# The S5 products of a hybrid decoder layer: from the accumulators to two spare banks, as one block behind each dense tile

## The chip, the cores and the metric

The kernel runs on one core of one Trainium2 chip. Its time is the device time of one execution in microseconds. Before the change the median of three runs is 2421.3 us (2419.39 to 2423.79). The engines are TensorE (PE), VectorE (DVE), ScalarE (ACT), GpSimd (POOL) and SyncE (SP, which here only issues DMAs). Each works off its own queue in order, and they meet by semaphores.

## The reference

One inference step of a two-layer decoder trunk over 1024 prompt rows and 8 x 4 sample rows, 1056 columns in all (T), model width 1024. Layer 0 is the even one, which the change concerns:

```python
p = rmsnorm(x, g_norm) @ w_in                      # q, k, v, g, a_lr, u
log_a = log_sigmoid(a_lr @ w_a2 + b_a2) / 16
o, s_gla = gla_chunked(q, k, v, log_a, s_gla)      # 4 heads
o = rmsnorm(o, g_head) * silu(g)
# S5: 32 groups of 16 channels, 64 complex states each
bu = einsum('bsgc,gpc->bsgp', u, bb)               # complex
h  = scan(h[t] = ab * h[t-1] + bu[t])              # complex, along the sequence
y  = Re(einsum(h, c)) + d_skip * u
z = gelu(y); z = z * sigmoid(z @ w_glu + b_glu)
x = x + concat([o, z]) @ w_out
x = x + square(relu(rmsnorm(x, g_mlp) @ w_up)) @ w_down
```

Layer 1 has a gated RG-LRU in the mixer's place, and the same MLP.

## The kernel before, in words

Everything lies with channels on the 128 partitions and the 1056 columns along the free axis. A dense product is done in three passes on two rounded halves of each operand (XH, XL for the activations, WH, WL for a weight tile of 128 x 1024): `product` runs 8 k steps x 3 column chunks of 352 x 3 passes, 72 matmuls, into one of two accumulators of three banks each (`acc[:, t % 2]`). Names are numbered in the table ACC; tile t may start when t - 2 has been read (`claim`). The weight tiles come in the order of the table STREAM; for each, ScalarE copies the raw tile to WH (`hi(n)`) and VectorE subtracts to get WL (`lo_w(n)`), which TensorE awaits. Two further banks, `ms`, are spare.

The even layer projects u0 to u3, q0, q1, g0 to g3, k0, k1, alr and the three tiles v0 to v2 (these with 512 columns; k runs over four weight tiles, n = 13 to 16). The S5 part works on four groups q = 0 to 3 of eight channel groups each, between the dense tiles. For each group: `build_xa` on VectorE, `step_ab` on TensorE (8 transposes and 12 products of 32 columns) which ScalarE reads to WIN and T7 (`read_ab`); `load_m`, eight small DMAs that spread T7 to M; `step_cd` (16 half-array products of 136 columns), read by `read_cd`; `core` on VectorE, the scan itself, with the angle tables built by `build_angles` and turned to sine and cosine by `turn_table`; `build_wo`; `step_ef` (24 products of 136 columns), read by `read_ef` to G. Then y goes out to DRAM (`store_y`), comes back turned (`turn_y`, eight DMAs), ScalarE does the GELU into TT[:, 2] and SP stores z (`z_out`). Both `decay` steps, which make the GLA decays out of the logits lg0 and lg1, wait on VectorE for `z_out` of all four groups and on ScalarE for the g stores. After them VectorE runs a long series of steps up to `pair_carried(0)`, then the weight tiles 17 and 18 and the low halves of z, which the first GLU tile on TensorE waits for. ScalarE's queue is written out by hand, as are VectorE's and TensorE's; their order sets what waits for what.

## Time and profile before

| | |
|---|---|
| median of 3 runs | 2421.3 us (2419.39 to 2423.79) |
| profiled execution | 2420.45 us, span 2418.6 us |
| mean granted TensorE clock | 0.956 of full |
| TensorE busy | 2337.1 us, 97% of the span |
| VectorE busy | 1188.8 us, 49% |
| ScalarE busy | 648.9 us, 27% |

The profile is of one execution, times counted from its first instruction. PE is TensorE's matmul row; a line such as L488 is that of a helper that many steps share, so steps are told apart by the tiles that they write and read (acc<-U,WIN is cd, ms or acc<-U,M opens ef, cst,XA is ab's transposes). The clock is given as a share: 1.00 is 2.4 GHz and 0.50 is 1.2 GHz. A number in brackets at a row's end is the idle time of the engine ahead of it, with what ended it. Some matmul records are missing from the trace.

### The profile page before, as it was taken

How to read it: one execution, taken by the hardware profiler on the slowest of the kernel's cores; microseconds unless marked ns; L12 is line 12 of the kernel's file. 1: busy time of each engine (PE TensorE's matmuls, PEld its weight loads, DVE VectorE, ACT ScalarE, POOL GpSimd, SP SyncE). 2: the span in 40 equal slices, each digit the busy share in tenths (PEclk: the TensorE clock that was granted, in tenths of full speed). 3: DMA queues.
4: the chain of work that ended last, by engine and by line, in shares of the span. 5: the costliest groups of instructions: out<-in, count | busy, mean ns of one | idle time of the engine just before them, and what ended most of it. 6: DMA issues, size and time to landing. Idle time of an engine off the chain costs nothing.

```text
span 2418.6 us, 32428 instructions
## 1 busy us (share of the span) xinstructions
PE 2337.1 (97%) x14010; PEld 2263.1 (94%) x14010; DVE 1188.8 (49%) x1324; ACT 648.9 (27%) x708; POOL 21.0 (1%) x35
## 2 busy tenths in 40 slices
PE   7999979989999999999999999999999999999997
PEld 6988768789999999999999888899999999999996
DVE  7874545234434434444446866624444444344344
ACT  5232432133211111112113544614211111111113
POOL 0000000000000000000000000000000000000001
PEclk9988985599999999999999999999999999999999
DMA  4343110131111111111111111111111111111112
GB/s 158 99 111 104 71 44 19 35 118 44 48 49 46 39 52 43 43 52 43 43 52 36 49 40 48 33 52 44 44 43 52 43 43 52 44 43 37 51 34 72
DMA packets 66087, 131.62 MB, mean 54 GB/s; under 512 B 24400, under 2 KB 37344, under 8 KB 66016
## 3 DMA queue, kind: packets, MB, share of 16 engines
q1 hardware_dynamic: 60256, 114.88, 14.7%
q0 software_dynamic: 3312, 12.06, 1.5%
q10 hardware_dynamic: 2448, 3.64, 0.5%
q8 instruction: 56, 0.92, 0.2%
q14 instruction: 15, 0.12, 0.0%
HBM read 114.66 MB, written 14.71 MB: 53 GB/s over the span
## 4 chain that ended last, share of the span: by engine, by line
PE 90%; DVE 5%; ACT 2%; issue 1%; DMA 1%; SPq 0%; DVEq 0%; ACTq 0%
PE acc L488 84%; PE acc L689 2%; DVE TT L1344 1%; PE acc L700 1%; PE acc L704 1%; PE ms L488 1%; ACT TT L1018 0%; DMA X<-in_x_t 0%; DVE XP L1344 0%; DVE XL L1347 0%; ACT L1018 0%; PE acc L712 0%; DVE WL L1344 0%; DMA p<-in_par 0%; PE acc L744 0%
## 5 line engine op out<-in xcount | busy, mean ns | idle before, releaser
L488 PE MATMUL acc<-XH,WH 128*128 128x352 f32 x2664 | 865.2, 325 | 37.8 <-DVE XL L1347 17.5
L488 PE MATMUL acc<-XH,WL 128*128 128x352 f32 x2664 | 858.5, 322 | 0.0
L488 PE MATMUL acc<-XL,WH 128*128 128x352 f32 x2664 | 856.7, 322 | 0.0
L1344 DVE TENSOR_TENSOR X<-X,acc 128x1056 f32<-128x1056 f32 (+1 forms) x288 | 343.3, 1193 | 419.4 <-PE acc L488 404.8
L488 PEld LDWEIGHTS acc<-XH,WH 128*128 128x128 f32 x2664 | 501.8, 188 | 45.5 <-issue 26.7
L488 PEld LDWEIGHTS acc<-XL,WH 128*128 128x128 f32 x2664 | 504.5, 189 | 0.0
L488 PEld LDWEIGHTS acc<-XH,WL 128*128 128x128 f32 x2664 | 501.4, 188 | 0.0
L488 PE MATMUL acc<-HH,WH 128*128 128x352 f32 x1536 | 496.6, 323 | 1.4 <-DVE X L1344 1.4
L488 PE MATMUL acc<-HH,WL 128*128 128x352 f32 x1536 | 495.9, 323 | 0.0
L488 PE MATMUL acc<-HL,WH 128*128 128x352 f32 x1536 | 495.3, 322 | 0.0
L919 ACT ACTIVATE WH<-WR 128x1024 fp32r<-128x1024 f32 x179 | 184.8, 1048 | 668.8 <-PE acc L488 608.8
L488 PEld LDWEIGHTS acc<-HH,WH 128*128 128x128 f32 x1536 | 288.5, 188 | 3.1 <-issue 1.7
L488 PEld LDWEIGHTS acc<-HL,WH 128*128 128x128 f32 x1536 | 288.3, 188 | 1.3
L488 PEld LDWEIGHTS acc<-HH,WL 128*128 128x128 f32 x1536 | 288.6, 188 | 0.0
L1347 DVE SCALAR_TENSOR_TENSOR TT<-acc,RS 128x1056 f32<-128x1056 f32 x64 | 80.5, 1258 | 418.8 <-PE acc L488 410.3
L1242 ACT ACTIVATE HH<-TT 128x1056 fp32r<-128x1056 f32 x64 | 69.6, 1087 | 584.5 <-DVE TT L1347 584.5
L1344 DVE TENSOR_TENSOR WL<-WR,WH 128x1024 fp32r<-128x1024 f32 x179 | 215.9, 1220 | 20.0 <-ACT WH L919 19.6
L1344 DVE TENSOR_TENSOR HL<-TT,HH 128x1056 fp32r<-128x1056 f32 x64 | 80.3, 1255 | 72.3 <-ACT TT L1245 72.3
L1245 ACT ACTIVATE TT<-TT 128x1056 f32<-128x1056 f32 x64 | 68.4, 1069 | 0.0
L926 ACT ACTIVATE TT<-X 128x1056 f32<-128x1056 f32 x24 | 25.9, 1081 | 126.7 <-DVE X L1344 126.7
L689 PEld LDWEIGHTS acc<-QM,KX 128*128 128x128 f32 x256 | 57.3, 336 | 1.3 <-DVE KX L1756 1.3
L689 PE MATMUL acc<-QM,KX 128*128 128x32 f32 x256 | 55.5, 393 | 1.0 <-DVE KX L1756 1.0
(314 smaller groups left out, 1356.4 us busy)
## 6 DMA issues: line engine op xcount, KB each, us to landing
WR<-in_w_stream SPq DMA_DIRECT2D x156, 512.0 KB, 3.2
WR<-in_w_stream POOLq DMA_DIRECT2D x23, 512.0 KB, 3.6
X<-in_x_t SPq DMA_DIRECT2D x16, 528.0 KB, 9.2
out_y_t<-X SPq DMA_DIRECT2D x12, 352.0 KB, 2.4
u_scratch<-UR SPq DMA_DIRECT2D x4, 576.0 KB, 3.0
U<-u_scratch SPq DMA_DIRECT2D x32, 72.0 KB, 2.7
y_scratch<-G SPq DMA_DIRECT2D x4, 544.0 KB, 2.8
VH<-y_scratch SPq DMA_DIRECT2D x32, 68.0 KB, 2.6
```

What stands on the lines that cost most here:

```text
L488: return pe.matmul(out, lhs, rhs, start=start, stop=stop)
L689: last = pe.matmul(glb[:, b, i * 2 * BL:(i + 1) * 2 * BL], KX[:, b, i * GC:(i + 1) * GC], QM[p][:, at:at + 2 * BL], start=True, stop=True)
L700: pe.matmul(glb[:, 2 + b, 0:2 * GC], S[:, p, :], QI[p][:, c * 2 * GC:(c + 1) * 2 * GC], start=True, stop=False)
L704: last = pe.matmul(glb[:, 2 + b, e * GC:(e + 1) * GC], V[:, c, h * P:(h + 1) * P], SC[:, b, e * GC:(e + 1) * GC], start=(c == 0), stop=(c ...
L919: act.activation(WH[:, n % SLOTS, :], WR[:, n % RAW, :], ACT.Copy).then_inc(w_hi, 1)
L926: act.activation(TT[:, (k - 1) % 3 if k else 3, :], X[:, k, :], ACT.Square).then_inc(sq_done, 1)
L1242: act.activation(HH[:, slot, :], TT[:, u, :], ACT.Square).then_inc(h_sq, 1)
L1245: act.activation(TT[:, 2 + u, :], TT[:, u, :], ACT.Square).then_inc(h_sq, 1)
L1344: return dve.tensor_tensor(out, a, b, op)
L1347: return dve.scalar_tensor_tensor(out=out, in0=a, scalar=scalar, in1=b, op0=op0, op1=op1)
```

## The change

All S5 products now write the two spare banks `ms` and no accumulator. Since these hold less, each step is done in two rounds, ab in t (transposes) and r (the 32-column products), cd and ef in a and b; the table S5R numbers the rounds, `s5_done` and `s5_read` count them, and each round waits until ScalarE has read the one ahead of it. The products of a step stand as one block behind the last matmul of a dense tile (`beside`). Never more than one block stands behind a tile: ab0 behind u3, cd0 behind g0, ab1 behind q1, cd1 behind k0, ef0 behind g1, ab2 behind k1, cd2 with ef1 behind g2, ab3 behind g3, cd3 with ef2 behind alr, and ef3 behind v0. k0 and k1 are projected earlier, v0 ahead of the logits, and the queues of VectorE and ScalarE follow. The four angle tables become two that alternate, and the range reduction has two parts of 2 pi instead of three. The functions step_ab, step_cd and step_ef are gone.

```diff
-STREAM = index(["u0", "u1", "u2", "u3", "q0", "g0", "q1", "g1", "g2", "g3", "k0", "k1", "alr",
+STREAM = index(["u0", "u1", "u2", "u3", "q0", "g0", "q1", "k0", "g1", "k1", "g2", "g3", "alr",
...
-ACC = index(["u0", "u1", "u2", "norm0", "u3", "ab0", "q0", "cd0", "ab1", "g0", "cd1", "q1", "ef0", "g1", "ab2", "ef1",
-             "cd2", "g2", "ab3", "ef2", "cd3", "g3", "k0", "ef3", "k1", "alr", "lg0", "lg1", "v0", "v1", "v2",
-             "glu0", "glu1", "glu2", "glu3",
+ACC = index(["u0", "u1", "u2", "norm0", "u3", "q0", "g0", "q1", "k0", "g1", "k1", "g2", "g3", "alr",
+             "v0", "lg0", "lg1", "v1", "v2", "glu0", "glu1", "glu2", "glu3",
+S5R = index(["ab0t", "ab0r", "cd0a", "cd0b", "ab1t", "ab1r", "cd1a", "cd1b", "ef0a", "ef0b", "ab2t", "ab2r",
+             "cd2a", "cd2b", "ef1a", "ef1b", "ab3t", "ab3r", "cd3a", "cd3b", "ef2a", "ef2b", "ef3a", "ef3b"])
...
+            K = sb(area, "K", [P, 2, T])
-                PTR = sb(s5b, "PTR", [P, 2, 12, NC])
-                VH1 = sb(s5b, "VH1", [P, 2 * PQ * 144])
-            K = sb(area, "K", [P, 2, T])
-            LA = sb(area, "LA", [P, 2, T])
+                LA = sb(s5b, "LA", [P, 2, T])
+            PT1 = sb(area, "PT1", [P, 2, PQ, NC])
+            VH1 = sb(area, "VH1", [P, 2 * PQ * 144])
...
-                    done_wait(sp, f"ef{q - 2}")
+                    s5_done_wait(sp, f"ef{q - 2}b")
-                read_wait(sp, f"ab{q}")
+                s5_read_wait(sp, f"ab{q}r")
-                    done_wait(sp, f"ef{q - 1}")
+                    s5_done_wait(sp, f"ef{q - 1}b")
-                read_wait(sp, f"ef{q}")
+                s5_read_wait(sp, f"ef{q}b")
...
+                    if k == ks[-1]:
+                        last.then_inc(acc_done[t % 2], 1)
+                if beside is not None:
+                    for k in ks:
+                        beside(k)
...
+            def claim_s5(name):
+                if S5R[name]:
+                    pe.wait_ge(s5_read, S5R[name])
+            def ab_part(q, i):
+                g = i % PQ
+                rows = [XA[:, r, g, :, :].rearrange("p l c -> p (l c)") for r in range(2)]
+                if i == 0:
+                    pe.wait_ge(xa_ready, q + 1)
+                    claim_s5(f"ab{q}t")
+                if i < PQ:
+                    for r in range(2):
+                        last = pe.transpose(ms[:, r, g * P:(g + 1) * P], rows[r], ident)
+                else:
+                    if i == PQ:
+                        claim_s5(f"ab{q}r")
+                    out = ms[:, 0, g * 32:(g + 1) * 32]
                     mm(out, ident, skip[:, 2 * g:2 * g + 2, :].rearrange("p e c -> p (e c)"), True, False)
                     for r in range(2):
+                        last = mm(out, rows[r], CB[:, r, PQ * q + g, :], False, r == 1)
+                if g == PQ - 1:
+                    last.then_inc(s5_done, 1)
+            def cd_part(q, n):
+                if n == 0:
+                    pe.wait_ge(u_in[q % 2], 16 * L * (q // 2 + 1))
+                    s5_read_wait(pe, f"ab{q}t")
+                    claim_s5(f"cd{q}a")
+                if n == 6:
+                    claim_s5(f"cd{q}b")
+                r, j = n // PQ, n % PQ
+                for e in range(2):
+                    h = 64 * e
+                    last = mm(ms[h:h + 64, n // 3 % 2, n % 3 * YW:(n % 3 + 1) * YW], WIN[:, r, j, h:h + 64],
+                              U[:, q % 2, 2 * j + e, NB:NB + YW], True, True)
+                if n in (5, 7):
+                    last.then_inc(s5_done, 1)
+            def ef_part(q, g):
+                if g == 0:
+                    pe.wait_ge(m_in, 16 * L * (q + 1))
+                    pe.wait_ge(st_ready, q + 1)
+                    pe.wait_ge(wo_ready, q + 1)
+                    claim_s5(f"ef{q}a")
+                if g == 4:
+                    claim_s5(f"ef{q}b")
+                h, at = 64 * (g % 2), g % 4 // 2 * YW
+                out = ms[:, g % 2, at:at + YW]
+                mm(out, M[:, g, :, :].rearrange("p l c -> p (l c)"), U[:, q % 2, g, 0:YW], True, False)
                 for r in range(2):
+                    last = mm(out, WO[h:h + 64, r, g // 2, :, :].rearrange("p l c -> p (l c)"),
+                              HV(q)[h:h + 64, r, g // 2, 0:YW], False, r == 1)
+                if g % 4 == 3:
+                    last.then_inc(s5_done, 1)
+            def cd_ef(q):
+                def part(k):
+                    for i in (2 * k, 2 * k + 1):
+                        if k < 4:
+                            cd_part(q, i)
+                        else:
+                            ef_part(q - 1, i - 8)
+                return part
             def logits(p):
...
+            project("u3", "u3", beside=lambda k: ab_part(0, k))
             project("q0", "q0")
-            step_cd(0)
-            step_ab(1)
-            project("g0", "g0")
-            step_cd(1)
-            project("q1", "q1")
-            step_ef(0)
-            project("g1", "g1")
-            step_ab(2)
-            step_ef(1)
-            step_cd(2)
-            project("g2", "g2")
-            step_ab(3)
-            step_ef(2)
-            step_cd(3)
-            project("g3", "g3")
-            project("k0", "k0")
-            step_ef(3)
-            project("k1", "k1")
-            project("alr", "alr")
+            project("g0", "g0", beside=lambda k: cd_part(0, k))
+            project("q1", "q1", beside=lambda k: ab_part(1, k))
+            project("k0", "k0", beside=lambda k: cd_part(1, k))
+            project("g1", "g1", beside=lambda k: ef_part(0, k))
+            project("k1", "k1", beside=lambda k: ab_part(2, k))
+            project("g2", "g2", beside=cd_ef(2))
+            project("g3", "g3", beside=lambda k: ab_part(3, k))
+            project("alr", "alr", beside=cd_ef(3))
+            values((0,), beside=lambda k: ef_part(3, k))
             read_wait(pe, "alr")
             logits(0)
             logits(1)
-            values()
+            values((1, 2))
...
+                s5_done_wait(act, f"ab{q}t")
+                act.activation(WIN[:, :, :, :].rearrange("p r g n -> p r (g n)"), ms[:, :, :], ACT.Copy).then_inc(s5_read, 1)
+                s5_done_wait(act, f"ab{q}r")
                 if q:
                     act.wait_ge(m_in, 16 * L * q)
-                act.activation(T7[:, :], acc[:, t % 2, 2, 0:P], ACT.Copy).then_inc(acc_read[t % 2], 1)
+                act.activation(T7[:, :], ms[:, 0, 0:P], ACT.Copy).then_inc(s5_read, 1)
...
+                for half in range(2):
+                    s5_done_wait(act, f"ef{q}{'ab'[half]}")
+                    if q and half == 0:
+                        act.wait_ge(y_out, 16 * q)
+                    act.activation(G[:, 4 * half * YW:4 * (half + 1) * YW].rearrange("p (j e n) -> p e j n", e=2, n=YW),
+                                   ms[:, :, 0:2 * YW].rearrange("p e (j n) -> p e j n", n=YW), ACT.Copy).then_inc(s5_read, 1)
...
-            gelu(2)
-            done_wait(act, "g3")
-            hi(13)
-            silu(3)
-            done_wait(act, "k0")
-            hi(14)
-            read_ef(3)
-            done_wait(act, "k1")
-            hi(15)
-            gelu(3)
             done_wait(act, "alr")
             hi(16)
+            gelu(2)
+            read_ef(3)
+            read_values(0)
+            gelu(3)
+            act.wait_ge(z_done, NG)
             act.wait_ge(g_out, 16 * 4)
             decay(0)
             decay(1)
...
+            read_values(1)
+            pair_decays(0)
+            pair_rest(0)
+            for i in range(2):
+                act.wait_ge(v_free, i + 1)
+                hi(17 + i)
+            read_values(2)
...
             build_xa(3)
-            lo_w(11)
-            build_wo(2)
             core(2)
             read_g(2)
-            build_angles(3)
-            lo_w(12)
+            build_wo(2)
+            lo_w(14)
+            read_g(3)
+            lo_w(15)
+            core(3)
+            read_row("alr", ALR, 16)
             build_wo(3)
-            core(3)
-            read_g(3)
-            lo_w(13)
-            read_row("k0", K[:, 0, :])
-            lo_w(14)
-            read_row("k1", K[:, 1, :])
-            lo_w(15)
-            read_row("alr", ALR, 16)
             lo_w(16)
-            read_wait(dve, "alr")
```

TensorE behind the tile g1 before; cst,XA are ab2's transposes, skip and CB its small products, U,M and VH,WO ef1:

```order
L565 MATMUL acc<-cst,XA 128x128 [waits acc_read0,xa_ready]
L565 MATMUL acc<-cst,XA 128x128 x7
L488 MATMUL acc<-skip,cst 128x32
...
L488 MATMUL acc<-U,M 128x136 [waits acc_read1,wo_ready,acc_read0,st_ready,m_in]
L488 MATMUL acc<-VH,WO 128x136 x2
...
L488 MATMUL acc<-U,WIN 64x136 [waits acc_read0,u_in0]
L488 MATMUL acc<-U,WIN 64x136 x15
```

and now, ab2 behind the tile k1, up to the dense tile g2:

```order
L584 MATMUL ms<-cst,XA 128x128 [waits s5_read,xa_ready]
L584 MATMUL ms<-cst,XA 128x128 x7
L496 MATMUL ms<-skip,cst 128x32 [waits s5_read]
L496 MATMUL ms<-CB,XA 128x32 x2
...
L496 MATMUL acc<-XH,WH 128x352 [waits acc_read1,w_ready]
```

ab2 stands alone between two dense tiles, and its second half has a wait of its own for the read of the first.

TensorE behind the last projection, alr, before: the logits (UR,wa), then v0 (the first row of 128x512):

```order
L488 MATMUL acc<-UR,wa 128x352 [waits acc_read0,wa2_in,acc_read1]
L488 MATMUL acc<-UR,wa 128x352 x2
L488 MATMUL acc<-UR,wa 128x352 [waits acc_read1]
L488 MATMUL acc<-UR,wa 128x352 x2
L488 MATMUL acc<-WH,XH 128x512 [waits w_ready,acc_read0]
```

and now behind v0: the second half of ef3, the logits, and v1:

```order
L496 MATMUL ms<-U,M 128x136 [waits s5_read]
L496 MATMUL ms<-VH,WO 128x136 x2
...
L496 MATMUL acc<-UR,wa 128x352 [waits acc_read1,wa2_in]
L496 MATMUL acc<-UR,wa 128x352 x2
L496 MATMUL acc<-UR,wa 128x352 [waits acc_read0]
L496 MATMUL acc<-UR,wa 128x352 x2
L496 MATMUL acc<-WH,XH 128x512 [waits acc_read1]
```

ef3 moved from between k0 and k1 to right ahead of the logits, v0 ahead of both.

ScalarE ahead of the decays before: L1024 is the GELU of y, L919 a weight tile's WH, L1018 the first decay's read of lg0:

```order
L1024 ACT_TABLE_LOAD [waits z_out]
L1024 ACTIVATE TT<-VH 128x8x128 [waits y_in]
L1025 ACTIVATE TT<-VH 128x4x8
L919 ACTIVATE WH<-WR 128x1024 [waits w_first0,acc_done1]
L1018 ACTIVATE TT<-acc,par 128x1056 [waits acc_done0,g_out]
```

and now: L1028 are the two reads of ef3, L1105 that of v0, L1048 the GELU, L1042 the read of lg0:

```order
L1028 ACTIVATE G<-ms 128x2x2x136 [waits y_out,s5_done]
L1028 ACTIVATE G<-ms 128x2x2x136 [waits s5_done]
L1105 ACTIVATE V<-acc,rs_col 128x512 [waits col_read,acc_done0]
L1105 ACTIVATE V<-acc,rs_col 128x512 x2
L1048 ACTIVATE TT<-VH 128x8x128 [waits z_out,y_in]
L1049 ACTIVATE TT<-VH 128x4x8
L1042 ACTIVATE TT<-acc,par 128x1056 [waits acc_done1,g_out,z_done]
```

The last GELU moved from ahead of the last weight tile to right behind ef3's reads, with the decay's first step directly behind it.

## Rows read from the trace of the kernel before

**Rows 1.** The page, parts 1 and 4: busy times, and the chain that ended last by engine

```profile
PE 2337.1 (97%) x14010; PEld 2263.1 (94%) x14010; DVE 1188.8 (49%) x1324; ACT 648.9 (27%) x708; POOL 21.0 (1%) x35
...
PE 90%; DVE 5%; ACT 2%; issue 1%; DMA 1%; SPq 0%; DVEq 0%; ACTq 0%
```

**Rows 2.** Windows: length, busy us (x instructions) of PE, PEld, DVE, ACT, POOL, clock, DMA

```profile
91.18:101.42 10.24, 9.84 (x43) 9.87 (x44) 9.83 (x13) 1.19 (x2) 0.00 (x0) 0.50 0.31 100
149.21:166.28 17.07, 17.07 (x70) 13.31 (x71) 7.60 (x11) 7.99 (x11) 0.53 (x1) 0.50 0.46 142
183.34:200.41 17.07, 17.07 (x74) 13.22 (x73) 9.40 (x15) 6.20 (x9) 0.53 (x1) 0.50 0.26 96
319.88:323.29 3.41, 3.31 (x11) 3.34 (x12) 3.41 (x4) 3.39 (x4) 0.00 (x0) 0.50 0.00 0
101.42:258.44 157.02, 155.68 (x925) 141.98 (x924) 94.17 (x130) 47.04 (x56) 4.49 (x9) 0.89 0.35 97
```

**Rows 3.** The chain of waits: start us, us, what

```profile
133.56 11.64 PE acc L488 x72
...
232.39 23.10 PE acc L488 x144
...
315.68 1.82 ACT V L1163 x3
```

**Rows 4.** Timeline of PE: start us, us, instruction, operands, count [idle before <-releaser]

```profile
69.93 1.04 PE L565 MATMUL acc<-cst,XA 128*128 128x128 f32 x8
...
91.58 1.94 PE L565 MATMUL acc<-cst,XA 128*128 128x128 f32 x8 [4.49 <-DVE Q L1344]
...
111.35 2.07 PE L488 MATMUL acc<-U,WIN 128*64 128x136 f32 x32
...
124.91 0.39 PE L488 MATMUL acc<-U,M 128*128 128x136 f32 x2
...
178.58 1.03 PE L565 MATMUL acc<-cst,XA 128*128 128x128 f32 x8
...
182.05 0.48 PE L488 MATMUL acc<-U,M 128*128 128x136 f32 x2
...
319.98 0.63 PE L488 MATMUL acc<-XH,WH 128*128 128x352 f32 x1 [4.33 <-DVE XL L1344]
```

**Rows 5.** Timeline of ACT

```profile
98.52 1.02 ACT L983 ACTIVATE WIN<-acc 128x1024 f32<-128x1024 f32 x1 [10.24 <-PE acc L488]
...
113.47 0.85 ACT L994 ACTIVATE VH<-acc 128x816 f32<-128x816 f32 x1 [0.96 <-PE acc L488]
...
246.44 2.19 ACT L1024 ACTIVATE TT<-VH 128x1024 f32<-128x1024 f32 x1
...
299.04 1.84 ACT L1163 ACTIVATE V<-acc,rs_col 128x512 f32<-128x512 f32 x3 [9.64 <-PE acc L488]
```

**Rows 6.** Timeline of SP, which issues DMAs

```profile
233.65 0.34 SPq L392 DMA_DIRECT2D y_scratch<-G  x1
236.38 3.63 SPq L398 DMA_DIRECT2D VH<-y_scratch  x8
```

**Rows 7.** DMA issues from 85 to 260 us: count, KB each, median us to landing

```profile
VH<-y_scratch SPq DMA_DIRECT2D x32, 68.0 KB, 2.6
...
z_scratch<-TT SPq DMA_DIRECT2D x4, 528.0 KB, 3.4
```

**Rows 8.** Timeline of DVE

```profile
91.35 1.22 DVE L1344 TENSOR_TENSOR G<-PT,VH 128x1024 f32<-128x1024 f32 x1
...
103.11 1.41 DVE L1344 TENSOR_TENSOR TT<-pw,p 128x512 f32<-128x512 f32 x2
...
107.46 1.23 DVE L1344 TENSOR_TENSOR WL<-WR,WH 128x1024 fp32r<-128x1024 f32 x1
...
260.50 0.71 DVE L1590 TENSOR_SCALAR TT<-TT 128x1056 f32<-128x1056 f32 x1 [2.62 <-ACT TT L1018]
...
294.86 2.49 DVE L1344 TENSOR_TENSOR QI<-QM,gs 128x1024 f32<-128x1024 f32 x2
```

More of the change, by code:

```diff
@@ L509, in product, with project @@
                         last.then_inc(x_free, 1)
[L510 removed]
+                    if k == ks[-1]:
[3 more added lines that the diff above has]
+                        beside(k)
             XOPS = (lambda k: XH[:, k, :], lambda k: XL[:, k, :])
[L514 removed]
+            def project(name, acc_name, xn=None, ks=None, free=False, beside=None):
                 n, t = STREAM[name], ACC[acc_name]
@@ L569, in step_ab @@
                     mm(out, ident, skip[:, 2 * g:2 * g + 2, :].rearrange("p e c -> p (e c)"), True, False)
                     for r in range(2):
-                        last = mm(out, XA[:, r, g, :, :].rearrange("p l c -> p (l c)"),
-                                  CB[:, r, PQ * q + g, :], False, r == 1)
-                last.then_inc(acc_done[t % 2], 1)
-            def step_cd(q):
-                t = ACC[f"cd{q}"]
-                pe.wait_ge(u_in[q % 2], 16 * L * (q // 2 + 1))
-                read_wait(pe, f"ab{q}")
-                claim(t)
-                for r in range(2):
-                    for g in range(GQ):
-                        h, n = 64 * (g % 2), r * PQ + g // 2
-                        last = mm(acc[h:h + 64, t % 2, n // 3, n % 3 * YW:(n % 3 + 1) * YW],
-                                  WIN[:, r, g // 2, h:h + 64], U[:, q % 2, g, NB:NB + YW], True, True)
-                last.then_inc(acc_done[t % 2], 1)
@@ L613, in logits, with values @@
                 last.then_inc(acc_done[t % 2], 1)
-            def values():
+            def values(tiles, beside=None):
                 n = STREAM["v0"]
-                for j in range(3):
+                for j in tiles:
                     t = ACC[f"v{j}"]
@@ L632, in values @@
                                 last.then_inc(v_free, 1)
-                    last.then_inc(acc_done[t % 2], 1)
+                            if b == 2 and k == KT - 1:
+                                last.then_inc(acc_done[t % 2], 1)
+                    if beside is not None:
+                        for k in range(KT):
+                            beside(k)
             project_pair(("u0", "u1"), ("u0", "u1"), SPLIT["norm0"])
@@ L1071, in _, with read_values @@
                 first_square(k)
+            def read_values(j):
+                t = ACC[f"v{j}"]
+                done_wait(act, f"v{j}")
+                act.wait_ge(col_read, 2)
+                for b in range(3):
+                    c = 3 * j + b
+                    n = GC if c < NGC else 32
+                    last = act.activation(V[0:n, c, :], acc[0:n, t % 2, b, :], ACT.Identity, scale=rs_col[0:n, c:c + 1])
+                last.then_inc(acc_read[t % 2], 1)
             def turn_table(q):
-                table = (PT0[:, :, :, :] if q == 0 else PTR[:, :, PQ * (q - 1):PQ * q, :])
+                table = (PT0, PT1)[q % 2]
                 act.wait_ge(angle_ready, q + 1)
@@ L1430, in reduce @@
                 link(dve.tensor_scalar(t, t, MAGIC, None, ALU.subtract))
-                for part in (TWO_PI_1, TWO_PI_2, TWO_PI_3):
+                for part in (TWO_PI_1, TWO_PI_2):
                     link(stt(x, t, -part, x, ALU.mult, ALU.add))
@@ L1529, in build_angles @@
                 shape = [P, PQ, NC]
-                table = (PT0[:, :, :, :] if q == 0 else PTR[:, :, PQ * (q - 1):PQ * q, :])
+                table = (PT0, PT1)[q % 2]
                 qs = slice(PQ * q, PQ * (q + 1))
@@ L1556, in core @@
                     dve.wait_ge(u_out, 16 * NG)
-                middle = middle or (lambda: None)
                 qs = slice(PQ * q, PQ * (q + 1))
                 four = [P, 2, PQ, NC]
-                pr, pi = [over((PTR[:, r, PQ * (q - 1):PQ * q, :] if q else PT0[:, r, :, :]).unsqueeze(1), four)
+                pr, pi = [over((PT0, PT1)[q % 2][:, r, :, :].unsqueeze(1), four)
                           for r in range(2)]
```

148 lines of the change are left out of this document (54 added, 94 removed).

## The prediction

> **What bounds the kernel now.** I read the page's busy times first: TensorE is busy 97% of the span of 2418.6 us, and the chain that ended last lies 90% on TensorE [rows 1]. So the time is TensorE's instructions, at the clock that they get, plus its waits. Only the even layer's mixer, the first 320 us, is touched. I took the granted clock in stretches next [rows 2]. In three stretches there, of 10.24, 17.07 and 17.07 us, the engine had 1.2 GHz instead of 2.4 GHz. The reader is to see what came before each: the first began about 4 us into a wait of TensorE that ended at 91.58, the third 4.76 us after the ab step that began at 178.58, with ef and cd behind it, and the second in the same way [rows 4]. Last I read the chain of waits and the timelines for the pieces' lengths. A dense tile (72 products of 352 columns) takes 23.10/2 = 11.55 us at the full clock and a tile of v (72 products of 512 columns) 315.68 - 299.04 = 16.64 us, from read to read [rows 3, 5]. From the end of u3 (69.93) to the end of alr (255.49) TensorE has one wait, of 4.49 us, that of ab1 [rows 3, 4]; behind that come v's three tiles, a wait of 4.33 us, and the first GLU tile at 319.98 [rows 4].
>
> I work between these two marks, 69.93 and 319.98, since behind 319.98 nothing is changed: by how much the GLU start moves, the end moves.
>
> **What goes.** Nine dense tiles are 104.0 us. The S5 work at the full clock is, for one group, ab 182.05 - 178.58 = 3.47, cd 2.07, and ef 133.56 - 124.91 = 8.65 us, together 14.2, and 56.8 for the four groups [rows 3, 4]. That makes 160.8 us, and the stretch took 185.6. The difference is 24.8. By the clock I would expect 22.2 for half of the 44.4 us, and 4.49 for the wait, of which 0.4 is in both: 26.3. I take the 24.8, since it is what the whole stretch shows. The wait goes: ab1 had to wait for VectorE's read of q0, since it took an accumulator; now it takes the spare banks, and g0 stands in front. If every S5 block stays at the full clock, all 24.8 go.
>
> **What comes: rounds.** Each S5 part now has two rounds through the same two banks, and the second waits until ScalarE has read the first. The bound from below is the read alone, from above the read plus both hand-overs and a busy ScalarE. Behind ab's transposes stands the 1024-column read, 1.02 us, and I take 1.3 us with 0.25 for the hand-overs; behind cd's first round 0.85 (816 columns), I take 1.05; behind ef's first round 544 columns, two thirds of that, 0.57 by proportion (an estimate), and I take 0.85 [rows 5]. In the two blocks that hold cd and ef, ef waits for cd's last read as well, 0.6. Sum: 4 x (1.3 + 1.05 + 0.85) + 2 x 0.6 = 14.0 us. The bounds are 10 (the reads alone, 4 x 2.44) and 20 (ScalarE late by a GELU of 2.19 us now and then [rows 5]). The ms banks have no second pair, so nothing runs beside these waits: the next dense tile is queued behind the block.
>
> The Trainium skill, "Trainium Kernel Development and Optimization", section "Best Practices", asks to double-buffer and to mind PSUM pressure, and reads steady bubbles as a sign that PSUM ran out. By it the single pair of banks is the price of the change, 14 us; by the row of the wait for q0 the shared accumulators cost 4.49 us before. The page names no duration, and my sum holds both.
>
> **What comes: v0.** VectorE's queue is cd3's read, core(3), alr's read, wo(3), WL of tile 16. Core is 103.11 - 91.35 = 11.76 us, wo 107.46 - 103.11 = 4.35, a read or a WL 1.2 each [rows 8]. So WL16 is ready 18.6 us behind cd3's last read, a hand-over with it. TensorE has ef2 (8.65 + 0.85) and the first six k of v0's first row block (4.15) to do there, 13.7 us. It waits 4.9 us; the bounds are 0 (ef2 at half clock covers it) and 7. What is queued behind is the whole rest of v0, ef3, the logits.
>
> Then v0 (16.64) stands ahead of ef3. The end of ef3 comes at 69.9 + 104.0 + 56.8 + 14.0 + 16.6 + 4.9 = 266.2 us.
>
> **What comes: the decays behind gelu(3).** This is the step on which I rest most. Before, ef3 ran between k0 and k1, and y's way through DRAM lay under k1 and alr. Now ef3 is the last thing ahead of the logits, and both decay(0) on ScalarE (its queue: read_ef(3), v0's read, gelu(3), then the decay) and decay(0) on VectorE (it waits for z_out) stand behind that way. Its length: ef's last read ends 0.75 us behind ef3's end. Before, the store went out at 233.65, right at that read's end, the turned loads from 236.38 to 240.01, and the last landed 2.6 later, 9.0 in all [rows 6, 7]. The GELU, 2.3 to 2.5 with its tail, and the store of z, 3.4 to landing, follow [rows 5, 7]. VectorE's decays so start 0.75 + 9.0 + 2.5 + 0.2 + 3.4 = 15.9 us (the 0.2 for the issue) behind ef3's end. From that start to the end of the carried queries it took 260.50 to 297.35, 36.85 us [rows 8]; two WL (2.4), then the first XL of z, as long as a WL (1.25), and TensorE starts 0.2 later: 40.7. ScalarE is about as late (exponentials, two halves, v2's read 1.84, a copy like WIN's 1.02) and no later. In the old kernel the v tiles hid this chain: from 260.50 on, 40.7 us end at 301.2, and TensorE was busy until 315.65. Now only v1 and v2 are left to hide it, 33.3 us, and v1 itself needs the accumulator that lg0 holds, which ScalarE reads only behind gelu(3), 13 us behind ef3's end. So TensorE is idle some 12 us ahead of v1 and some 7 to 10 ahead of the GLU tile, and the GLU start is 266.2 + 15.9 + 40.7 = 322.8.
>
> With the clock full everywhere that is 2.8 us later than 319.98. In one line: -24.8 (clock and wait) + 14.0 (rounds) + 13.6 (alr to GLU, 16.6 + 4.9 + 56.6 against 64.5) = +2.8.
>
> **What of the clock comes back.** An ef alone ran 8.65 us at the full clock. So did ab0, whose transposes took 1.04 us where those of ab1, at the low clock, took 1.94. In two blocks of ab, ef and cd the clock fell, and in the wait of 4.49 us [rows 2, 4]. The new blocks are shorter on the whole, but each has a hole of about a microsecond in it, and two of them (cd, ef) are 10.7 us of small products with three holes. I bound the return by 0 and by all 44.4 us at half the clock, 22 us, plus one of 3.41 us in each of the other blocks. I take one long stretch like the old ones (8.5 us lost), one of 3.41 us like that at 319.88 (1.7 lost) behind the wait in v0, and one more of that size at the GLU start, where the wait is now longer than 4.33: together 11.9. Clock lost in v1 or v2 costs nothing, since the chain above hides it.
>
> The Trainium skill, "TensorE: Matmul & The Clock Gate", section "Why this matters for your kernels", asks for no idle gaps between bursts and says that the gate then falls to half. The trace agrees for the 4.49 us gap, and the rule speaks against the 5, 12 and 8 us gaps that the change makes; of the S5 blocks it says nothing that I could price.
>
> One reduction step less in build_angles saves 0.7 us on VectorE four times and a little at the start; VectorE is late only in front of WL16, where none of it lies. Cost and gain nothing. Loading k0 and k1 earlier, and the two alternating tables (core(1) is through before angles(3), core(0) before angles(2)), cost nothing either: VectorE is busy 94 of the 157 us from 101.42 to 258.44 [rows 2]. If that cover failed, a dense tile would wait as long as an angle table, 7 us.
>
> **Sum.** +2.8 + 11.9 = +14.7 on the profiled execution's 2420.45 us, whose span is 2418.6. The median shown is 0.85 higher; 2421.3 + 14.7 = 2436.0 us.
>
> **Rivals.** About 0.2%, 4.8 us, is what a measurement of this kernel can tell from no change.
> (1) Full clock: the holes don't lower it, only the sum's +2.8 and the GLU start's 1.7 are left. For it: ef0 and ab0 alone didn't fall. Against it: holes inside them. 2424 to 2426, chance 0.22.
> (2) Faster: the end of ef3 decides. The chain behind it is fixed at 56.6 us, so ef3 must end before 263.3 for no loss and before 258.5 for a gain that can be told. That needs rounds at the lower bound (10 instead of 14) and no wait in v0 (core(3) shorter, -4.9), with no clock lost: ef3 ends at 257.3, and 2421.3 + 2.8 - 8.9 = 2415. For it: cover and reads are near each other. Against it: three good cases at once. Chance 0.08.
> (3) The clock falls in most blocks: four ab blocks at 1.7 to 3.4 and both long blocks at 8.5, with the rest as forecast: +2.8 + 10 + 17 + 1.7 + 1.7, part of it under the wait in v0: 2421.3 + 29 = 2450. For it: both old ab and ef pairs fell. Chance 0.18.
> (4) The change does not spread the blocks as it says (ScalarE stands in GELU or a table when a round wants it): rounds at 20, +6 on the forecast, 2442; inside my range, chance with the forecast.
> The forecast, between 5 and 24 us slower, has 0.52. The range reaches from 2420 to 2451 us. Faster by over 0.2% 0.08, within 0.2% 0.20, slower 0.72.
>
> **What would show it.** TensorE's timeline should show holes of about a microsecond inside each S5 block, put down to ScalarE's reads of ms; a wait of some 5 us in v0 for WL; a wait of about 12 us for ScalarE ahead of v1 and of 7 or more ahead of the first GLU tile. The SP queue should show the last y store some 30 us later than 233.65, and the chain of waits should run, behind ef3, through y's DMAs, the GELU, z's store and VectorE's decays. The GLU start should be at 330 to 340. I am wrong if v1 follows the logits without a gap, if ef3 ends before 258, or if the stretch up to alr has no stretch at half clock: the first two would make it faster, the third would leave no change.

## The result, and the profile after

The changed kernel takes 2444.15 us (median of 4 runs, 2441.23 to 2446.34) against 2421.75 us of the kernel before (4 runs, 2419.39 to 2423.79). The ratio is recorded as 1.0102, with a 95% interval from 1.0084 to 1.0119; the two medians divided give 1.0092. One of e7's seven executions below, of 2894.08 us, was in a slower state of the chip and is left out of its numbers. The forecast was 2436.0 us in a range from 2420 to 2451: the sign and the range held, the time came out 8 us above the forecast.

The profiled execution has a span of 2440.5 us instead of 2418.6. The page shows no more work on TensorE, only a lower share of it:

```profile
PE 2343.6 (96%) x14010; PEld 2268.2 (93%) x14010; DVE 1185.8 (49%) x1318; ACT 646.0 (26%) x701; POOL 21.1 (1%) x35
...
PE 89%; DVE 5%; ACT 3%; issue 1%; DMA 1%; SPq 0%; DVEq 0%; ACTq 0%
```

Against [rows 1] the 14010 products are the same number, busy 6.5 us longer, and DVE and ACT have 6 and 7 instructions fewer. So the 21.9 us of span are waits and clock. The waits of PE between 40 and 345 us are these (line, releaser: us in total, times, longest):

```profile
PE acc L496 <- DVE XL L1370: 7.0, 1, 7.0
PE acc L496 <- ACT TT L1042: 5.1, 1, 5.1
PE ms L496 <- ACT WIN L1007: 4.5, 4, 1.1
PE ms L496 <- ACT VH L1018: 3.8, 4, 1.0
PE ms L496 <- ACT G L1028: 2.9, 4, 0.7
PE acc L496 <- DVE WL L1370: 1.5, 1, 1.5
PE ms L496 <- ACT VH L1021: 1.2, 2, 0.6
```

The four rows with ms are the rounds: 4.5 + 3.8 + 2.9 + 1.2 = 12.4 us in 14 holes, each put down to ScalarE's read of the spare banks. The first two rows stand behind ef3, and WL is the wait in v0.

The clock is the larger thing. These are all the stretches at half clock from 69 us to the GLU tile (the columns are those of [rows 2]):

```profile
72.72:79.55 6.83, 6.83 (x29) 6.83 (x29) 5.55 (x11) 3.30 (x5) 0.00 (x0) 0.50 0.35 121
120.51:123.92 3.41, 3.41 (x14) 3.41 (x13) 3.38 (x4) 0.96 (x2) 0.53 (x1) 0.50 0.01 2
154.64:164.88 10.24, 10.24 (x35) 8.99 (x34) 4.84 (x7) 2.54 (x3) 0.00 (x0) 0.50 0.32 113
178.53:181.95 3.42, 3.42 (x14) 3.42 (x14) 0.00 (x0) 3.24 (x3) 0.00 (x0) 0.50 0.02 6
202.43:212.67 10.24, 10.24 (x34) 8.98 (x35) 9.79 (x15) 3.94 (x4) 0.00 (x0) 0.50 0.27 83
226.32:229.73 3.41, 3.41 (x13) 3.41 (x13) 0.00 (x0) 3.38 (x3) 0.00 (x0) 0.50 0.02 5
250.21:257.04 6.83, 6.83 (x21) 5.10 (x20) 6.51 (x11) 2.47 (x3) 0.00 (x0) 0.50 0.16 64
280.93:301.41 20.48, 15.33 (x36) 9.81 (x36) 1.61 (x2) 6.88 (x8) 0.00 (x0) 0.50 0.26 82
335.55:345.79 10.24, 5.45 (x19) 5.48 (x20) 9.25 (x8) 7.62 (x9) 1.59 (x3) 0.50 0.28 102
```

Before, [rows 2] had three stretches ahead of alr's end and some tens of microseconds without any. (A fourth, from 258.44 to 268.68, lay in the logits and v0.) Now the engine falls to 1.2 GHz eight times ahead of the end of ef3: during or just behind each of the four ab, and in each of the four ef. The timeline of ef0 shows one fall as it happens (start us, us, instruction, [idle before <-releaser]):

```profile
151.66 0.73 PE L496 MATMUL ms<-VH,WO 64*128 64x136 f32 x4
153.10 0.50 PE L496 MATMUL ms<-U,M 128*128 128x136 f32 x2 [0.71 <-ACT G L1028]
...
154.19 0.50 PE L496 MATMUL ms<-U,M 128*128 128x136 f32 x2
154.62 1.27 PE L496 MATMUL ms<-VH,WO 64*128 64x136 f32 x4
```

The reader is to see the hole of 0.71 us, 1.5 us of products at the old pace behind it, and then the same four products in 1.27 us instead of 0.73. The first half of this ef took 4.31 us, the second 6.69. The old ef0, the same products without the hole, took 8.65 us in all [rows 3, 4].

The sum by marks. Ef3 ends at 285.7, and the GLU tile starts at 340.34 instead of 319.98, 20.4 us later. Of the remaining 1.5 us of the span about 1.1 is clock right behind that mark: 5.45 us at half clock (340.34 to 345.79) where the kernel before had 3.31 (319.98 to 323.29). The half clock ahead of ef3's end adds up to 49.2 us (the seven first rows, and 4.8 of the eighth), so 24.6 us lost. On TensorE's timeline these three rows follow, the logits' products, the first of v1 and the first of the GLU tile:

```profile
285.69 7.40 PE L496 MATMUL acc<-UR,wa 16*128 16x352 f32 x12
```
```profile
298.23 0.79 PE L496 MATMUL acc<-WH,XH 128*128 128x512 f32 x1 [5.15 <-ACT TT L1042]
...
340.34 0.63 PE L496 MATMUL acc<-XH,WH 128*128 128x352 f32 x1 [7.01 <-DVE XL L1370]
```

Behind it the chain runs as it was forecast. SP sends y at 286.44 and the turned loads from 289.16 (before: [rows 6]), ACT's GELU and the first read of the logits follow, and DVE starts its decays when z has landed:

```profile
286.44 0.34 SPq L400 DMA_DIRECT2D y_scratch<-G  x1
289.16 3.63 SPq L406 DMA_DIRECT2D VH<-y_scratch  x8
297.03 0.34 SPq L423 DMA_DIRECT2D z_scratch<-TT  x1
```
```profile
294.91 2.04 ACT L1048 ACTIVATE TT<-VH 128x1024 f32<-128x1024 f32 x1 [6.76 <-DMA VH<-y_scratch]
...
297.04 1.14 ACT L1042 ACTIVATE TT<-acc,par 128x1056 f32<-128x1056 f32 x1
```
```profile
299.76 0.71 DVE L1614 TENSOR_SCALAR TT<-TT 128x1056 f32<-128x1056 f32 x1 [38.25 <-DMA z_scratch<-TT]
...
334.14 2.48 DVE L1370 TENSOR_TENSOR QI<-QM,gs 128x1024 f32<-128x1024 f32 x2
...
338.94 4.76 DVE L1370 TENSOR_TENSOR XL<-TT,XH 128x1056 fp32r<-128x1056 f32 x4
```

From 299.76 to the end of the carried queries it is 36.86 us; [rows 8] gave 36.85. VectorE is what TensorE waits for here, and it stood idle for 38.25 us just before.

### The profile page after: what moved, and what is told of

Its sections match the earlier page's. It is cut to its first block, busy times and chain, and to the rows that moved or that the text cites. A ratio compares the mean times of both kernels' runs of the same rounds, so it can differ in the third digit from the quotient of the medians.

```text
span 2440.5 us, 32419 instructions
## 1 busy us (share of the span) xinstructions
PE 2343.6 (96%) x14010; PEld 2268.2 (93%) x14010; DVE 1185.8 (49%) x1318; ACT 646.0 (26%) x701; POOL 21.1 (1%) x35
## 4 chain that ended last, share of the span: by engine, by line
PE 89%; DVE 5%; ACT 3%; issue 1%; DMA 1%; SPq 0%; DVEq 0%; ACTq 0%
PE acc L496 81%; PE ms L496 3%; PE acc L714 2%; DVE TT L1370 1%; PE acc L725 1%; PE acc L729 1%; ACT TT L1042 1%; DMA X<-in_x_t 0%; DVE XP L1370 0%; ACT L1042 0%; PE acc L737 0%; DVE XL L1373 0%; DMA p<-in_par 0%; PE acc L769 0%; PE acc L760 0%
```

## The experiments

**Theory:** two mechanisms, nearly independent. (A) The holes that the rounds put into the blocks of small products make TensorE's clock fall, so the S5 part costs more than its waits. (B) The decays stand behind gelu(3), and the chain behind ef3 is longer than v1 and v2 can hide. **Rivals:** the old clock loss has nothing to do with the holes and would come back however the products are spread (C); or the chain costs nothing, since TensorE is late anyway. The kernel before was run again beside each experiment, with medians of 2419.16 to 2420.19 us against the 2421.75 beside the changed kernel, so a difference between the medians of two experiments is good to some 2 us at best.

**e1: the S5 products spread between the dense ones.** The same two banks and the same rounds, but a part of a block is issued behind each k step of the dense tile; one table and two SiLUs on ScalarE go behind the reads that the rounds want. (Not shown here: the same for v0's tile, and ScalarE's order.)

```diff
                     if k == ks[-1]:
                         last.then_inc(acc_done[t % 2], 1)
-                if beside is not None:
-                    for k in ks:
-                        beside(k)
+                    if beside is not None:
+                        beside(k)
...
```

> The changed kernel, with each part of an S5 block put behind its own k step of the dense tile (nine dense products stand between two parts) and not behind the whole tile; three of ScalarE's sine and SiLU steps come behind its read of ms. Same products, same banks, same rounds. Theory A (the waits for ScalarE's reads inside a block both cost time and make the clock fall): the reads lie beside 1.4 us of dense products, so the waits of 12 us and most of the eight stretches at half clock in front of ef3's end (285.75 us) go. ef3 ends at about 250, the GLU start at 250 + 54.6 = 305, and the time is about 2444 - 36 = 2408 us. Rival C (the small products themselves, wherever they stand, lower the clock): only the waits go, the half clock stays at some 45 us, the time is about 2432 us.

Measured: 2423.07 us (10 runs), ratio to before 1.0017 (1.0006 to 1.0027), 21 us less than the changed kernel. The clock behaved as theory A says; these are the windows from 69 us to the first fall, and that fall, the only one ahead of ef3's end:

```profile
69.00:173.00 104.00, 99.94 (x649) 90.96 (x648) 76.88 (x111) 22.85 (x29) 3.17 (x6) 1.00 0.36 95
173.18:176.60 3.42, 3.42 (x16) 3.06 (x17) 0.59 (x1) 2.79 (x4) 0.00 (x0) 0.50 0.41 163
```

But the time missed theory A's by 15 us. The waits tell half of it:

```profile
PE acc L496 <- ACT TT L1040: 7.0, 1, 7.0
...
PE ms L496 <- DMA U<-u_scratch: 6.3, 2, 4.2
```

TensorE comes to cd2 at 169 instead of 192 us, and its operand U has not landed; with cd3 that is a new wait of 6.3 us, and the one fall of the clock begins at 173.18, just behind its first 4.22 us. The other half is the price of spreading. In a spread tile one step of cd and nine dense products take 119.71 - 117.69 = 2.02 us, where nine dense products take 11.55/8 = 1.44 and an eighth of cd's block 2.07/8 = 0.26 [rows 3, 4]; the timeline of e3 below, whose products stand in the same order, shows two such steps:

```profile
117.30 0.45 PE L496 MATMUL ms<-U,WIN 128*64 128x136 f32 x4
117.69 0.43 PE L496 MATMUL acc<-XH,WH 128*128 128x352 f32 x1
...
119.32 0.45 PE L496 MATMUL ms<-U,WIN 128*64 128x136 f32 x4
119.71 0.43 PE L496 MATMUL acc<-XH,WH 128*128 128x352 f32 x1
```

The step costs 0.32 us more than its parts; 16 such steps in cd0 and cd1 and 8 double ones (0.3 each) in cd2 and cd3 are some 7.5 us. A step of ef with its nine dense products shows none of it (135.87 - 133.35 = 2.52 from one ef part to the next, and 1.44 + 8.65/8 = 2.52). That it is the change of the products' shape is a guess; no run isolates it. So the rounds' waits went (12.4 to 1.1), the clock came back (24.6 to 1.7 lost), and 6.3 + 7.5 were given back: 285.7 - 11.3 - 22.9 + 6.3 + 7.5 = 265.3; by the timeline ef3 ends at 265.2. What of it the chain behind ef3 keeps for itself is e3's question.

**e2: the decays ahead of gelu(3).** The placement of the S5 products is the changed kernel's. Some buffers change their places, so that the decays share nothing with y's last group, and VectorE's decays wait for three stores of z instead of four.

```diff
...
-            gelu(3)
-            act.wait_ge(z_done, NG)
             act.wait_ge(g_out, 16 * 4)
             decay(0)
             decay(1)
+            act.wait_ge(lg_dve, 4)
+            gelu(3)
...
-            dve.wait_ge(z_out, 16 * NG)
+            dve.wait_ge(z_out, 16 * (NG - 1))
...
```

> The changed kernel, with both decays ahead of the last GELU on ScalarE, and VectorE's decays waiting for three stores of z and not four; some tiles lie elsewhere in SBUF for that. Nothing else. Theory (what stands behind ef3 is the chain y store, turned loads, GELU, z store, decays): the decays start about 3.5 us behind ef3's end and not 14; TensorE's wait of 5.15 us ahead of v1 goes to 3 or less, the GLU start comes from 340.3 to about 330, and the time is about 2434 us. Rival (the chain would be hidden anyway, v1 and v2 at half clock are the bound): within 3 us of 2444.

Measured: 2434.44 us (4 runs), ratio 1.0060 (1.0043 to 1.0076), as expected: by the medians this edit is worth 9.7 us (the intervals leave some 5 us of doubt). The rows of the rounds are the same to 0.1 us, the wait for ScalarE ahead of v1 has gone, and that ahead of the GLU tile is back at its old size [rows 4]:

```profile
PE acc L496 <- DVE XL L1370: 4.3, 1, 4.3
PE ms L496 <- ACT VH L1018: 3.8, 4, 0.9
```

The decays start at 294.89, 5.3 us behind ef3's end (289.6) instead of 14.1; 3.5 was expected. From ef3's end to the GLU start (337.02, where some 330 was expected) it took 47.4 us instead of 54.6. The profiled execution moved less than the medians (span 2437.0, 3.5 us less), since it lost more clock than that of the changed kernel: 63.2 us at half clock ahead of ef3's end instead of 49.2, 7 us. Single executions of these kernels differ that much in where the clock falls, so I take prices from the medians. The differences are telling. Its blocks stand as in the changed kernel, with the same holes, yet ab1's hole of 1.11 us (117.11) had no fall behind it, the clock being full from 79.77 to 151.45; and in cd2 with ef1 the clock fell at 195.82, behind cd's holes of 0.95 and 0.59 us and 7.3 us ahead of the end of ef1's own.

**e3: both.** The edits of e1 and of e2 in one kernel.

> Both edits together: S5 parts behind k steps, and decays ahead of the last GELU. If both theories hold the gains add up: ef3's end at about 250, the GLU start at about 250 + 44 = 294, the time about 2444 - 46 = 2398 us, faster than the kernel before by 23. If the clock does not recover, 2422.

Measured: 2414.08 us (10 runs), ratio 0.9974 (0.9964 to 0.9984), so 30.1 us less than the changed kernel and 0.26% less than the kernel before. The parts alone were 21.1 and 9.7 us, 30.8 together: within the some 5 us that the intervals leave open, the two edits add. The expected time was again too low by what e1 had shown, the wait for U (6.7 us here) and cd's steps.

**e4: a hole in each ef of the kernel before.** The counter-test of A: nothing of the change, but TensorE waits in the middle of ef until ScalarE has read the first four groups.

```diff
                 for g in range(GQ):
+                    if g == 4:
+                        last.then_inc(ef_half, 1)
+                        pe.wait_ge(ef_read, q + 1)
                     h, at = 64 * (g % 2), g // 2 * YW
...
```

> The kernel before, with one edit: in each of the four ef steps TensorE waits behind the fourth group until ScalarE has read the first four. Products, accumulators and order are as before. In the kernel before, ef0 (124.91 us) and ef3 (223.73 us) ran alone behind a dense tile at the full clock. Theory A (the hole makes the clock fall): each of these two now has a stretch at half clock, two falls more, and ef0's second half takes about 6.5 us and not 4.35; the end moves by about 4 x 0.75 + 2 x 4 = 11 us. Rival B (it is the place or the banks, not the hole): no new fall in ef0 and ef3, and the end moves by 3 us.

Measured: one run of 2433.77 us, span 2432.0. Ef0 and ef3 of the kernel before had run at the full clock. With a hole of 0.71 us in each, both fall:

```profile
129.63 0.50 PE L489 MATMUL acc<-U,M 128*128 128x136 f32 x2 [0.71 <-ACT G L1006]
```
```profile
131.86:138.69 6.83, 6.83 (x23) 5.83 (x23) 3.77 (x6) 2.03 (x4) 0.00 (x0) 0.50 0.20 79
...
237.67:247.91 10.24, 10.23 (x32) 8.24 (x33) 0.00 (x0) 0.75 (x3) 0.00 (x0) 0.50 0.15 59
```

In the kernel before the windows of ef0 and of ef3, each from its start into the dense tile behind it, read:

```profile
124.91:136.00 11.09, 11.09 (x65) 8.99 (x65) 10.17 (x18) 3.44 (x5) 0.00 (x0) 1.00 0.04 14
223.73:235.00 11.27, 11.27 (x66) 9.16 (x66) 2.39 (x2) 2.26 (x4) 0.53 (x1) 1.00 0.18 65
```

That is the cleanest evidence in the study: same accumulators, same order of products, same placement, one hole more, one fall more, twice, in one profiled execution of each kernel (the first of ScalarE's three reads of ef becomes two). It does not say that a fall needs a hole: in the kernel before, ef1 and ef2, which stood right behind ab and had no hole, fell at 149.21 and 183.34 [rows 2], 0.7 and 1.3 us behind their starts. The time of e4 is not a price of the clock: ScalarE was late in the second and third ef (waits of 3.08 and 6.09 us), so TensorE's waits for G are 10.6 us, and the GLU start moved by 331.33 - 319.98 = 11.35. Ef0's second half took 6.1 us, where 6.5 was expected and 4.35 was the old length.

**e5: a hole in each ab of the kernel before.** TensorE waits behind ab's transposes until ScalarE has read them; the read of ab0 goes ahead of a copy and a table.

```diff
+                last.then_inc(ab_half, 1)
+                pe.wait_ge(ab_read, q + 1)
...
```

> The kernel before, with one edit: in each ab step TensorE waits behind the eight transposes until ScalarE has read them to WIN (and at ab0 this read comes ahead of two other things on ScalarE). In the kernel before, ab0 (69.93 us) stood alone behind a dense tile, at the full clock, and the changed kernel fell there (72.72 us). Theory A (the hole makes the clock fall): a stretch at half clock begins within some 4 us of ab0's start; the end moves by 2 to 3 us for it and 1.1 for each of the four holes, if ScalarE is free, more where it isn't. Rival B (ab fell in the changed kernel for another reason, the banks or ScalarE's queue): the clock is full up to 91 us as before.

Measured: one run of 2435.77 us, span 2434.0. The answer is mixed. Ab0 with a hole of 1.18 us now falls at 73.82, where the kernel before had no fall until 91; ab1 with a hole of 1.13 us does not, and the whole stretch around it is at 2.4 GHz:

```profile
73.82:80.64 6.82, 6.82 (x27) 6.82 (x27) 5.49 (x12) 4.54 (x7) 0.00 (x0) 0.50 0.31 106
90.00:97.00 7.00, 5.87 (x66) 5.45 (x63) 5.16 (x6) 3.09 (x5) 0.53 (x1) 1.00 0.54 173
```

The other two ab got longer holes, since ScalarE was late (5.24 and 2.14 us), and were followed by long stretches at half clock, but the kernel before had falls there too. So a hole in ab can make the clock fall and need not. The time moved by more than the 7 us or so that was expected, since the four waits are 9.7 us and not 4.4, and the long stretches at half clock grew from 17.07 us each to 23.89 and 20.48.

**e7: the changed kernel with ab's hole covered.** The transposes are issued behind the fifth k step, the small products behind the tile as before; ScalarE reads within the three k steps between. The rounds of cd and ef are unchanged; ScalarE reads ab2 and ab3 ahead of a SiLU each, not behind it.

```diff
                     if k == ks[-1]:
                         last.then_inc(acc_done[t % 2], 1)
+                    if early and k == 4:
+                        for i in range(PQ):
+                            beside(i)
...
```

> The changed kernel, with one edit: the transposes of each ab come behind the fifth k step of the dense tile, its small products stay behind the whole tile. ab's four holes go (4.5 us of waits), cd's and ef's stay. Theory A: the four stretches at half clock that began in ab blocks (72.72, 120.51, 178.53, 226.32; 17.1 us, so 8.5 lost) go too, those of ef stay, and the time is 2444 - 13 = 2431 us. Rival (the small products of 32 columns lower the clock without a hole): only the waits go, 2439.5 us.

Measured: 2430.7 us (6 runs), ratio 1.0054 (1.0036 to 1.0073), 13.4 us less than the changed kernel; by the two ratios it is 11.6, give or take 6. Of the eight falls, the four behind ab are gone and the four of ef are all still there:

```profile
64.40:95.30 30.90, 30.90 (x205) 30.66 (x203) 23.20 (x39) 5.83 (x8) 1.58 (x3) 1.00 0.62 176
147.85:154.68 6.83, 6.83 (x25) 6.08 (x24) 4.07 (x6) 1.57 (x2) 0.00 (x0) 0.50 0.28 89
188.81:199.05 10.24, 10.24 (x35) 8.49 (x34) 9.79 (x15) 1.57 (x2) 0.00 (x0) 0.50 0.18 60
233.18:243.42 10.24, 10.24 (x31) 7.71 (x31) 9.79 (x15) 2.85 (x3) 0.00 (x0) 0.50 0.17 58
263.90:287.79 23.89, 18.91 (x45) 12.60 (x45) 1.97 (x2) 7.74 (x9) 0.00 (x0) 0.50 0.23 70
```

The waits lose just one row, that of WIN with its 4.5 us. In the changed kernel the four ab falls were 6.83 + 3.41 + 3.42 + 3.41 = 17.1 us, 8.5 lost: 4.5 + 8.5 = 13.0, and 13.4 was measured. Ef3 ends at 271.0 instead of 285.7, with 34.4 us at half clock ahead of it instead of 49.2. So a hole cost its own length and about twice that in clock, the proportion of e1 too (11.3 of waits and 22.9 of clock). Two things changed together here, though: the hole went, and the transposes moved away from the products of 32 columns. E7 refutes that these products alone lower the clock; that it is the hole and not the longer block rests on ab0 of the kernel before (no hole, no fall) against ab0 of e5.

**e6: e3 with U loaded first.** The wait for U in e3 has a plain cause: in SyncE's queue the loads of M and the turned loads stand ahead of it. In e6 the U loads follow the y store directly.

> e3_both with the loads of U for group q + 2 issued right behind the store of y, ahead of the loads of M and of the turned y. In e3_both TensorE waited for U at cd2 and cd3, 6.7 us in all, and the clock fell at each (174.03, 214.99). If the place in the SP queue is the cause, both waits go and with them about 3 us of half clock: 2414 - 9 = 2405 us. Rival (ScalarE's or VectorE's queue is late at the same places, or the chain behind ef3 is the bound): 2411 to 2414.

Measured: 2415.11 us (10 runs), ratio 0.9989 (0.9976 to 1.0003): no gain over e3. The wait did not go, it changed its name:

```profile
PE ms L496 <- ACT VH L1016: 7.7, 2, 4.7
```

Now the turned loads are last, gelu(0) waits for them until 174.10 (170.23 in e3), and ScalarE reads cd2 only behind gelu(0) and a table.

**e8: U between M and the turned loads, and the read of cd3 ahead of silu(3).**

```diff
                 if q + 1 < NG:
                     load_m(q + 1)
-                turn_y(q)
                 if q + 2 < NG:
                     load_u(q + 2)
+                turn_y(q)
...
```

> Both changes of e3 (S5 products between the dense products, decays ahead of gelu(3)), and in SyncE's queue the loads of U stand behind the loads of M and ahead of the turned loads; ScalarE reads cd3 ahead of silu(3). In e3 TensorE waited 4.00 and 2.74 us for U, since the turned loads stood ahead of it; in e6, with U ahead of M, it waited 4.70 and 3.05 us for ScalarE, which stood in gelu(0) and gelu(1) behind the turned loads, those now last. If each wait was the queue's order alone (theory), both go here: U lands about 166.5, ahead of 168.8, and the turned loads still land by 171, so that gelu(0) ends about 173 and the read of cd2 is not late. The 6.7 us of waits go and with them the stretches at half clock behind them (2 to 3 us lost): 2405 to 2409 us, with ef3's end near 260. If SyncE's queue is simply full in that stretch and one of its users is always late (rival), the time stays at that of e3 and e6, 2412 to 2416, and TensorE waits some 4 and 3 us for ScalarE's read ms->VH again.

Measured: 2409.69 us (6 runs), ratio 0.9962 (0.9948 to 0.9976), 0.7 us above the theory's interval and below the rival's, and by half of the mechanism. At cd3 nothing waits any more; at cd2 the rival is right, and ScalarE is late again:

```profile
PE ms L496 <- ACT VH L1016: 5.1, 1, 5.1
...
PE ms L496 <- DMA U<-u_scratch: 0.2, 1, 0.2
```

The loads M, U and y take 6.56, 6.60 and 4.09 us to issue one behind the other from 153.01 to 170.40, and TensorE is through with the dense products that follow cd2's first round at 175.6: the queue issued without a pause there, as the rival says, and the turned loads landed only at 174.19, when gelu(0), which stands ahead of the read of cd2, could start. E8 is the fastest kernel of the study, 34 us below the change as made and 0.38% below the kernel before. TensorE is at the full clock from 69 to 267 us but for one stretch of 6.83 us.

## Why the prediction came out as it did

**The sign was right, and for the right reason.** The forecast had the GLU start at 330 to 340 and TensorE waiting for ScalarE ahead of v1 and for VectorE ahead of the GLU tile. Both waits are there, the start is at 340.34, just beyond, and e2 shows that taking the last GELU out of the decays' way is worth 9.7 us. The chain measured 54.6 us from ef3's end to the GLU start, against 56.6: 14.1 instead of 15.9 up to VectorE's decays, and 40.6 instead of 40.7 from there. The last y store came 53 us later than 233.65 and not some 30: 33 by the forecast's own end of ef3 at 266.2, 10.2 of clock that it counted but left out of this mark, and 9.3 by which ef3 ended later than 276.4.

**The step that was mis-sized is the term "what of the clock comes back": 11.9 us.** Of it 10.2 lay ahead of ef3's end; it was 24.6. This is rival 3's mechanism, which had a chance of 0.18 and a time of 2450 us, nearer to the 2444.15 than the forecast was. Spreading the products took 22.9 us of it away (e1); that the holes do it is shown for ef (e4), and for ab by e7 with one of e5's two clean cases. The argument for a small term was that an ef alone and ab0 alone had run at the full clock and that the new blocks are shorter. Both were true and beside the point: what was new was the hole in the middle, and no block of the kernel before had one. The forecast said so itself, and then priced the blocks by their length. The 24.8 us that it took out first were a real loss of the old blocks, which had no holes, and of the wait for q0; but as much, 24.6 us, came back in the new blocks.

**The rounds:** forecast 14.0, measured 12.4 (1.11 behind the transposes against 1.3, 0.95 against 1.05, 0.71 against 0.85, 0.59 against 0.6). Read plus hand-over was the right model; a hand-over is about 0.1 us, not 0.25. But by e1 and e7 a hole costs about three times its length, and that was missing.

**The wait in v0:** forecast 4.9, measured 1.50. The lower bound's reason held: ef2 and v0's first products ran partly at half clock and so covered VectorE. The same lost microseconds must not be counted twice.

**The wait ahead of v1:** forecast some 12, measured 5.15. ScalarE began to read lg0 11.3 us behind ef3's end instead of 13, nearly as forecast, but the logits' twelve rows took 7.40 us, all at half clock, and the forecast gave them about one (in e3, at the full clock, six of them took 2.04 us); the trace of before had 5.84, most of it at half clock:

```profile
256.81 5.84 PE L488 MATMUL acc<-UR,wa 16*128 16x352 f32 x12 [1.34 <-DVE UR L1344]
```

**By the sum:** the forecast's 266.2 and 10.2 of clock make 276.4 for ef3's end. Clock +14.4, waits -5.0 (13.9 instead of 18.9), and u3's end at 69.4 instead of 69.9, give 285.3; it was 285.7. With the chain 2.0 shorter the GLU start comes at 322.8 + 10.2 + 9.3 - 2.0 = 340.3. So a term that was 14.4 us too small shows as 7.3, since others were too large. Some of that is no luck, as the lost clock itself filled 3.4 us of the wait in v0 (ef2 and v0's start had 6.83 us at half clock); the rest, some 4 us, is.

**What was put at nothing.** The shorter reduction and the alternating angle tables cost nothing that shows: no wait of TensorE between 40 and 345 us names a table. No run tried them alone.

**The other rivals.** Full clock (1) is refuted by the windows. Faster (2) named ef3 before 258.5 as its point: even e3 and e8, with the clock back, ended it at 267.3 and 263.9; they became faster because e2's edit had moved the point, so that the chain no longer decided. Late ScalarE (4) didn't happen in the changed kernel (no round waited over 1.11 us), but it did in e4, e5, e6 and e8.

The page "TensorE: Matmul & The Clock Gate" of the Trainium skill, section "Why this matters for your kernels", asks for no idle gaps between bursts, and means gaps longer than any that the rounds make. The forecast rightly took it as a word on the long gaps only. The trace agrees at the wait of 4.22 us in e1, which ended as the clock fell (173.18); behind that of 3.05 us in e6 no fall came, the clock being full from 185.15 to 270.48. On the short gaps it says nothing, and here falls came behind gaps of 0.71 us in ef (e4), and none behind one of 1.13 us in ab (e5) and those of 0.95 us in cd0 and cd1 (the changed kernel, e2, e7).

**Open.** Why one hole makes the clock fall and another doesn't is not settled: ab0 and ab1 of e5 have nearly the same hole and the same products. Ab1 has a fall behind its hole in the changed kernel and none in e2, with the same products in the same place, so part of it differs from execution to execution. I have no run that separates what stood ahead of them. Nor does any run say why ef behind ab fell without a hole in the kernel before. That cd's steps cost 0.3 us more among dense products and ef's do not is measured, its cause wasn't tried.

## What to carry to other kernels

Price a wait inside a run of small matrix products by the clock as well: here a microsecond of hole cost about three (e1, e7). Before you count a clock loss as saved, name what caused it, check that the change takes that away, and look for what the new blocks have that the old ones had not. When the last piece of a pipeline is moved later, follow all that is queued behind it to the first tile of the next stage: that length could be read off the old trace to 2 us, and what needn't wait for the piece can go ahead of it.

## What the runs showed of the hardware

A gap of 0.71 us in the middle of 8.65 us of products of 136 columns was followed by a fall to 1.2 GHz in thirteen of thirteen cases (four in the changed kernel, two in e4, four in e7, three in e2; in e2's fourth the clock had fallen 7.3 us before), 0 to 3 us behind the gap's end. In five of them cd with its own gaps stood right ahead. The same products without a gap, ef0 and ef3 of the kernel before, had none, and neither had the same products among dense ones from 69 to 173 us of e1; but ef1 and ef2 of the kernel before, behind ab and without a gap, fell.

A gap of 1.11 to 1.18 us behind ab's transposes was followed by a fall in eight of ten cases (four of four in the changed kernel, three of four in e2, one of two in e5).

A read of the spare banks by ScalarE costs TensorE its own duration and 0.1 us: 1.11 for 1.02, 0.95 for 0.85, 0.71 for 0.62.

The same small products have another price by their neighbours: an eighth of cd costs 0.26 us in a block and 0.58 among dense products, an eighth of ef the same in both.
